# A sample's query row spread over the partitions by one single-pass product instead of two passes or a full fp32 product

## The reference

```python
z = x @ w_in                       # q, k, v, gb, gc, h
att = attend(q, k, v)              # prompt: causal; samples: over a paged cache
mix = concat([att, gb * causal_dwconv(gc * h)]) @ w_out
x1 = layer_norm(ALPHA * x + mix)
up = causal_dwconv(x1 @ w_up); a, g = split(up)
y = layer_norm(ALPHA * x1 + (silu(a) * g) @ w_down)
```

## Time and profile before

| | |
|---|---|
| time, median of 3 runs | 447.54 us (446.76 to 448.65) |
| span of the profiled execution | 446.5 us |
| TensorE products | 416.1 us busy, 93% |
| TensorE weight loads | 341.0 us, 76% |
| VectorE | 296.0 us, 66% |
| ScalarE | 181.6 us, 41% |
| GpSimd | 104.4 us, 23% |
| moved by DMA | 124.85 MB, mean 280 GB/s |

### The profile page before, as it was taken

One profiled execution on the slowest core, in us unless ns is written; L12 is line 12 of the kernel. 1 busy time (PEld: TensorE's weight loads), 2 busy tenths in 40 slices (PEclk: granted clock), 3 DMA queues, 4 the chain that ended last, 5 costly groups with the idle time before them and its releaser, 6 DMA issues.

```text
span 446.5 us, 8259 instructions
## 1 busy us (share of the span) xinstructions
PE 416.1 (93%) x2911; PEld 341.0 (76%) x2911; DVE 296.0 (66%) x383; ACT 181.6 (41%) x694; POOL 104.4 (23%) x133
## 2 busy tenths in 40 slices
PE   4999999999999998999798989999999999999990
PEld 4588887876866774664364369999999999999990
DVE  0496999999799976944351264766666877534536
ACT  1476568653377334011110043455554456224201
POOL 1003033995255231100000436211222221000002
PEclk9999999999999999999999999999999999999997
DMA  8999999999999999999999953566666685968002
GB/s 294 385 329 386 385 388 379 370 357 390 398 386 372 351 393 387 386 386 386 386 377 386 304 166 111 159 178 189 189 182 170 166 215 155 234 174 212 24 1 97
DMA packets 109515, 124.85 MB, mean 280 GB/s; under 512 B 5775, under 2 KB 66920, under 8 KB 109466
## 3 DMA queue, kind: packets, MB, share of 16 engines
q1 hardware_dynamic: 101138, 107.55, 72.5%
q10 hardware_dynamic: 8336, 16.78, 10.5%
HBM read 121.90 MB, written 2.61 MB: 279 GB/s over the span
## 4 chain that ended last, share of the span: by engine, by line
PE 55%; DVE 18%; SPq 11%; issue 6%; DMA 5%; POOL 2%; ACT 1%; DVEq 0%; POOLq 0%; ACTq 0%
PE ps L1815 11%; PE ps L1816 11%; PE ps L1817 11%; SPq L354 8%; DVE qk L930 5%; DVE T L940 5%; PE ps L1432 4%; PE ps L1627 4%; PE ps L1708 3%; PE ps L1603 3%; PE ps L1629 3%; PE ps L1372 3%; DMA wring<-in_cache_v 2%; DMA KV<-in_cache_k 2%; POOL x1l L605 1%
## 5 line engine op out<-in xcount | busy, mean ns | idle before, releaser
L1177 DVE TENSOR_TENSOR wlo<-KV,whi 128x2048 fp32r<-128x2048 f32 (+1 forms) x24 | 61.8, 2576 | 57.1 <-ACT whi L832 29.1
L1432 PE MATMUL ps<-xT,wring 128*128 128x264 f32 x384 | 89.6, 389 | 0.0
L1432 PEld LDWEIGHTS ps<-xT,wring 128*128 128x128 f32 x384 | 71.9, 191 | 13.4 <-issue 1.7
L1815 PE MATMUL ps<-x1h,whi 128*128 128x264 f32 x256 | 73.8, 288 | 0.2
L930 DVE TENSOR_TENSOR qk<-KV,qk 128x1536 f32<-128x1536 f32 (+1 forms) x32 | 67.8, 2122 | 9.2 <-DMA KV<-in_cache_k 5.5
L1817 PE MATMUL ps<-x1h,wlo 128*128 128x264 f32 x256 | 72.7, 284 | 0.0
L1816 PE MATMUL ps<-x1l,whi 128*128 128x264 f32 x256 | 72.7, 284 | 0.0
L662 ACT ACTIVATE qk<-qk 128x64 f32<-128x64 f32 x216 | 51.8, 244 | 28.5 <-POOL qk L553 21.1
L940 DVE TENSOR_REDUCE T<-qk 128x24 f32<-128x1536 f32 (+1 forms) x32 | 58.4, 1827 | 0.0
L1815 PE MATMUL ps<-fh,whi 128*128 128x264 f32 x176 | 50.4, 286 | 0.1
L1816 PE MATMUL ps<-fl,whi 128*128 128x264 f32 x176 | 50.0, 284 | 0.0
(11 more groups left out here) (218 smaller groups left out, 578.9 us busy)
## 6 DMA issues: line engine op xcount, KB each, us to landing
KV<-in_cache_k SPq DMA_DIRECT2D x128, 256.0 KB, 7.3
KV<-in_w_ffn_up SPq DMA_DIRECT2D x32, 512.0 KB, 5.1
KV<-in_cache_v SPq DMA_DIRECT2D x60, 256.0 KB, 8.5
wring<-in_cache_v SPq DMA_DIRECT2D x56, 256.0 KB, 7.5
KV<-in_w_ffn_down SPq DMA_DIRECT2D x8, 1408.0 KB, 7.0
wring<-in_w_in ACTq DMA_DIRECT2D x5, 2048.0 KB, 15.1
zbuf<-in_cache_v SPq DMA_DIRECT2D x12, 256.0 KB, 6.0
zbuf<-in_w_ffn_up SPq DMA_DIRECT2D x3, 1024.0 KB, 11.5
```

Source lines behind the costliest of these rows:

```text
L1177: nc.vector.tensor_tensor(wlo[s][:, 0:n], w2[s][:, 0:n], whi[s][:, 0:n], ALU.subtract).then_inc(s_lo, 1)
L1432: ins = nc.tensor.matmul(ps[:, z_bank(n), 0:R], tile[k], xT[:, k, :], start=k == 0, stop=k == KT - 1)
L1815: nc.tensor.matmul(out, wh[k], xh[k], start=k == 0, stop=False)
```

## The change

The samples' query rows stand twice in the product's result: `xsP` gets the samples in columns 0 to 7 and again in 8 to 15, so that partition 32g + 8 + b of the result holds the same row as 32g + b. DVE rounds the whole to `qsr[:, 0]`, and then one operation makes `qsr[:, 1]` = `qsr[:, 0]` * m + result, with m = 0 in the first eight partitions of each 32 (the row, rounded) and m = -1 in the next eight (the rest). The selector picks partitions b and 8 + b together, so one single-pass product spreads rounded part and rest, for every sample. The fp32 copy `qs` is gone, ScalarE's wait for it too, the selector's rounding stands first, and PE waits for all three DVE operations ahead of the first product. The selector constant grows from 8 to 17 columns. `lnr` lies on `hT0`, and `ctail` has memory of its own.

```diff
-        lnr = sb("lnr", [16, P])
-        sel = sb("sel", [P, NS])
+        sel = sb("sel", [P, 2 * NS + 1])
+        lnr = at("lnr", nc.sbuf_base - 6 * P * 4, [16, P], F32)
-        qs = sb("qs", [P, DA])
-        qs_mem = nc.sbuf_base - DA * 4
-        ctail = at("ctail", qs_mem, [NTAIL, DA], F32)
+        ctail = sb("ctail", [NTAIL, DA])
...
-            act.wait_ge(s_qs, 1)
...
-            nc.vector.tensor_copy(xsP[:, :, 0:NS], ps[:, 6, 0:KT * NS].rearrange("p (k b) -> p k b", k=KT)).then_inc(s_xsP, 1)
+            nc.vector.tensor_copy(xsP[:, :, 0:2 * NS].rearrange("p k (r b) -> p k r b", r=2),
+                                  ps[:, 6, 0:KT * NS].rearrange("p (k o b) -> p k o b", k=KT, o=1).to_broadcast([P, KT, 2, NS]))\
+                .then_inc(s_xsP, 1)
+            dve.wait_ge(s_sel, 16)
+            nc.vector.tensor_copy(selr, sel[:, NS:2 * NS]).then_inc(s_qs, 1)
             dve.wait_ge(s_qsps, 1)
-            nc.vector.tensor_copy(qs, ps[:, 7, :]).then_inc(s_qs, 1)
             nc.vector.tensor_copy(qsr[:, 0, :], ps[:, 7, :]).then_inc(s_qs, 1)
             dve.wait_ge(s_qs, 2)
-            nc.vector.tensor_tensor(qsr[:, 1, :], ps[:, 7, :], qsr[:, 0, :], ALU.subtract).then_inc(s_qs, 1)
-            dve.wait_ge(s_sel, 16)
-            nc.vector.tensor_copy(selr, sel).then_inc(s_qs, 1)
+            nc.vector.scalar_tensor_tensor(qsr[:, 1, :], qsr[:, 0, :], sel[:, 2 * NS:2 * NS + 1], ps[:, 7, :], ALU.mult, ALU.add)\
+                .then_inc(s_qs, 1)
...
-            pe.wait_ge(s_qs, 1)
-            pe.wait_ge(s_sel, 16)
+            pe.wait_ge(s_qs, 3)
 
             def query(b):
                 if b >= 2:
                     pe.wait_ge(s_qb, b - 1)
-                if b < 2:
-                    nc.tensor.matmul(ps[:, 4 + b % 2, :], sel[:, b:b + 1].to_broadcast([P, P]), qs,
-                                     start=True, stop=True).then_inc(s_qbps, 1)
-                    return
-                pe.wait_ge(s_qs, 4)
-                pick = selr[:, b:b + 1].to_broadcast([P, P])
-                nc.tensor.matmul(ps[:, 4 + b % 2, :], pick, qsr[:, 0, :], start=True, stop=False)
-                nc.tensor.matmul(ps[:, 4 + b % 2, :], pick, qsr[:, 1, :], start=False, stop=True).then_inc(s_qbps, 1)
+                nc.tensor.matmul(ps[:, 4 + b % 2, :], selr[:, b:b + 1].to_broadcast([P, P]), qsr[:, 1, :],
+                                 start=True, stop=True).then_inc(s_qbps, 1)
...
-                ins = nc.tensor.matmul(ps[0:NS, 4 + c, :], sel, er[:, c, :], start=True, stop=True)
+                ins = nc.tensor.matmul(ps[0:NS, 4 + c, :], sel[:, 0:NS], er[:, c, :], start=True, stop=True)
...
-    pick = tok[:, None] % 32 == np.arange(NS)[None, :]
+    row = tok[:, None] % 32
+    rest = row // NS == 1
+    pick = np.concatenate([row == np.arange(NS)[None, :], (row < 2 * NS) & (row % NS == np.arange(NS)[None, :]),
+                           -rest.astype(np.float32)], 1)
```

## The result

The changed kernel took 439.99 us (median of 4 runs, 439.51 to 441.22), the kernel before beside it 448.1 us: ratio 0.983, 95% interval 0.9811 to 0.9849. That is 8.1 us faster, where 447.5 us and no change were forecast, and outside the range. The profiled execution has a span of 438.0 us against 446.5.

The account below looks back on a forecast made before the run. The prediction took DVE's chain, from the keys' landing at 36.9 us to the penalties near 103.4, as the bound, with PE's lead lost at 70.10: 446.5 + 0 + 1.0 = 447.5 us, range 445.6 to 449.2.

Parts of the forecast that it names:

- Bytes are as before: DMA: selector grows from 4 to 8.5 KB in the same 128 rows, lnr only lies elsewhere; no cost expected.
- DVE's chain: From the keys' landing at 36.86 us to 103.3: multiplies and reductions per four key pages, with hardly a gap.
- DVE in turn can't start sooner: DVE's stage begins when keys issued up to 27.97 us land, behind constants the change doesn't touch; gain 0.
- 0.45 was forecast: Start of the first z tile on PE: about 19.57 us instead of 20.02, bounded by the last xT copy.
- 1.38 forecast: Other six samples on PE, between z tiles: one product instead of a pair each, saving 6 x 0.23 us.
- PE's wait ahead of the key rows: At 70.10 us PE waits for ScalarE's copy of key rows; the wait was to grow from 1.06 to 2.9 us.
- from there on PE runs as before: After the longer wait at 70.10 us, PE's work was to go on unchanged, with gain 0 at the end.
- the sign of rival 1: PE's wait at 70 us staying near 1 us, with all behind it earlier.
- rival 1: PE is the bound and its saving lasts: 445.7 us, or 444.7 with the whole 2.84 us; chance 0.12.
- the 1.83 us: PE's lead at the end of the first four z tiles, 0.45 + 1.38, expected to be lost at 70.10 us.
- Rival 2: Earlier w_in load delays key pages from 36.9 us on, DVE waits: 448.2 us, at most 449.5; chance 0.15.
- Rival 4: GpSimd's operation no longer meets DVE's multiply near 41 us: 0.6 us less, 446.9 us; chance 0.10.

Follow-up runs that it names:

- e1: Kernel before with lnr on hT0 and 64 B free ahead of wo_att, so big tiles begin as in the changed kernel, old query work: 441.09 us, ratio 0.9849.
- e10: The kernel of e1 (changed kernel's layout, query work of the kernel before), measured again beside the changed kernel: 441.65 us, ratio 0.9859.
- e2: Changed kernel with 192 B free ahead of wo_att, big tiles at 192 modulo 256 as in the kernel before: 449.01 us, ratio 1.0022.
- e4: Changed kernel with 64 B free ahead of wo_att, big tiles at 64 modulo 256: 448.92 us, ratio 1.0023.
- e3: Changed kernel with 128 B free ahead of wo_att, big tiles at 128 modulo 256: 447.94 us, ratio 0.9993.

## Why the prediction was wrong

*The step that failed* is a single sentence of the part on DMA: "Bytes are as before", with the selector's growth and the lnr tile, which "only lies elsewhere". It took a moved tile to cost nothing. The diff shows 512 B leaving and 36 B coming (64 with the padding) ahead of the tiles that take nearly all of the loads. What this shifts is the start of some 90 MB of transfers up to 250 us, and with it the rate of the one resource that was full all that time, by 4.9% (386 to 405 GB/s). e1 shows it alone: 6.8 us (447.93 to 441.09), and in its repeat e10 6.0 us (447.69 to 441.65), of the 8.1. None of the four rivals spoke of addresses, so the range couldn't hold it.

*The bound.* That DVE's chain leads from the landing of the keys to the penalties was right in the changed kernel: its stage kept its length. But the prediction read the chain only to 104 us, where the change's work stops to matter, and said of some 250 us of full DMA slices only that they can't settle the bound alone. Behind the penalties the transfers set the end of the third stage, 5.8 us of the gain, and ahead of them the landing at 36.9, 2.35 us. "DVE in turn can't start sooner" held for the edits that it thought of, not for the rate.

*The parts of the query work* were close in size. The first three are read in the changed kernel, the last in e2, which has the old layout:

- A single-pass product costs 0.23 us, forecast and seen: two products and the next start take 22.98 - 22.33 = 0.65 us where four took 24.50 - 23.39 = 1.11.
- The scalar_tensor_tensor took 0.75 us, within 0.60 to 0.80, not the 0.69 taken. From DVE's first copy of the query rows to the first z tile it is 18.89 - 15.39 = 3.50 us against 20.02 - 16.20 = 3.82, a gain of 0.32 where 0.45 was forecast.
- Counted from the first z tile to the w_in load, 34.77 - 18.89 = 15.88 us against 37.23 - 20.02 = 17.21: 1.33 us, with 1.38 forecast.
- PE's wait ahead of the key rows, 2.9 us forecast, was 3.12 in e2, with the gain gone behind it: 449.01 us, ratio 1.0022, with 447.5 forecast for the query work by itself. But "from there on PE runs as before" failed: PE ran at half the clock for 6 us behind the wait and lost 2.8 us. In the changed kernel the wait stayed at 1.01 us, which the prediction had named as the sign of rival 1. It wasn't that: PE and DVE had both become early, PE by the query work and DVE by the rate.

*Rival 1* (PE's saving lasts, 445.7 or less) is false as put. In the new layout some 0.8 to 1.4 of the 1.83 us do last, for a reason that is open. *Rival 2* (keys come late) happened in e2 to e4, at another page than the one examined: 0.79, 0.82 and 0.61 us at 50 to 51 us. Its margin had been worked out for the page wanted at 54.15 only. *Rival 4* (GpSimd and DVE no longer meet) didn't happen: the multiply there took 2.80, 2.96 and 2.46 us in the changed kernel's three profiles, 2.92 before.

## What to carry to other kernels

When a diff adds, removes or resizes a tile, work out where the tiles behind it begin, before and after, and treat a change modulo 256 B of a tile that transfers fill as a change of its own. Where a page shows the DMA engines full at a rate that is flat from slice to slice, ask what sets that rate, not only what is queued. Measure such a side effect alone (a pad of 64 B is enough): otherwise 6.0 to 6.8 us are booked to an idea that is worth 0.8 to 1.4, or, with the tiles placed as before, nothing. And where a saving on one engine is forecast to turn into a longer wait of that engine, read its granted clock behind the wait: the lead may come back as a loss.

## What the runs showed of the hardware

- Transfers of 2048 B rows into SBUF ran at 404 to 405 GB/s when the rows began at multiples of 256 B and at 386 to 387 GB/s when they began 64, 128 or 192 B past one. The DMA share read 1.05 in both, so the share doesn't tell that a full stream is slower than it need be.
- The loss isn't proportional to the misplaced share. Against 405 GB/s it was 0 at 185 to 215 us with 16 of 44 pages and a 1 MB load misplaced, 4 with 28 of 44 pages (401), 12 with nearly all (393), and 18 to 19 with all (387 and 386).
- The part of the traffic that was well placed hid part of the loss of the other part: KV alone cost 2.25 us, wring alone 1.65, both together 6.75.
- TensorE's granted clock was 0.50 for 6 us in e2, e3 and e4, behind waits of 3.07 to 3.12 us, and PE lost 2.8 us by it in e2. In the changed kernel, with 1.01 us of waiting at the same place, it was 1.00 throughout.
